# A two-block transformer layer on one core: the first feed-forward upward product as seven block products, staged through DRAM

## What is computed

```python
h = rmsnorm(x, g_ffn[i])                                              # 1024 x 1024
x = x + jnp.square(jax.nn.relu(h @ w_ffn_up[i])) @ w_ffn_down[i]      # up 1024 x 4096, down 4096 x 1024
```

## Time and profile before

| | us |
|---|---|
| three runs without profile | 3553.3, 3554.5 (median), 3556.45 |
| profiled execution, from first to last instruction (its own device time isn't listed apart) | 3550.2 |
| TensorE busy | 3451.9 (97%) |
| VectorE, ScalarE, GpSimd busy | 1781.8, 1286.5, 1058.5 |
| merge's last products end, first upward product starts | 1186.0 |
| the last downward products of this stage end | about 1884 |

### The profile page before, as it was taken

The page is one execution under the profiler, slowest core; times in us unless marked ns, Lnnn a source line. Parts: engine busy times, 40 slices in busy tenths (PEclk is TensorE's granted clock), DMA queues, the critical chain, the costliest instruction groups (busy, mean ns, idle before and its releaser), DMA issues.

```text
span 3550.2 us, 48554 instructions
## 1 busy us (share of the span) xinstructions
PE 3451.9 (97%) x20382; PEld 2810.6 (79%) x20382; DVE 1781.8 (50%) x2379; ACT 1286.5 (36%) x2195; POOL 1058.5 (30%) x594
## 2 busy tenths in 40 slices
PE   7999999999999999999998899999999999999999
PEld 6888888887678888888887677777788788888887
...
GB/s 151 40 24 43 47 25 46 51 34 7 1 175 181 54 48 48 49 53 48 48 48 89 101 81 81 81 80 107 175 205 148 90 48 48 48 49 52 48 48 54
DMA packets 280073, 253.14 MB, mean 71 GB/s; under 512 B 11365, under 2 KB 221729, under 8 KB 279856
## 3 DMA queue, kind: packets, MB, share of 16 engines
...
...
## 4 chain that ended last, share of the span: by engine, by line


## 5 line engine op out<-in xcount | busy, mean ns | idle before, releaser
L414 POOL TENSOR_TENSOR weight_lo<-stage,weight_hi 128x1024 fp32r<-128x1024 f32 (+4 forms) x267 | 628.6, 2359 | 1389.4 <-ACT weight_hi L406 1360.9
L377 PE MATMUL psum<-hT_hi,weight_hi 128*128 128x512 f32 x2240 | 884.3, 395 | 5.7 <-DVE hT_lo L563 4.2
L378 PE MATMUL psum<-hT_lo,weight_hi 128*128 128x512 f32 x2240 | 873.5, 390 | 0.0
L379 PE MATMUL psum<-hT_hi,weight_lo 128*128 128x512 f32 x2240 | 873.1, 390 | 0.0
L377 PEld LDWEIGHTS psum<-hT_hi,weight_hi 128*128 128x128 f32 x2240 | 421.7, 188 | 103.5 <-issue 5.2
L378 PEld LDWEIGHTS psum<-hT_lo,weight_hi 128*128 128x128 f32 x2240 | 421.8, 188 | 90.0 <-issue 4.1
L379 PEld LDWEIGHTS psum<-hT_hi,weight_lo 128*128 128x128 f32 x2240 | 421.5, 188 | 88.3
L406 ACT ACTIVATE weight_hi<-stage 128x1024 fp32r<-128x1024 f32 (+4 forms) x329 | 316.5, 975 | 477.8 <-PE psum L379 441.8
L2096 DVE TENSOR_TENSOR x<-x,psum 128x512 f32<-128x512 f32 x416 | 279.8, 687 | 218.8 <-PE psum L379 218.2
L377 PE MATMUL psum<-weight_hi,act_hi 128*128 128x512 f32 x864 | 338.9, 392 | 0.0
L379 PE MATMUL psum<-weight_hi,act_lo 128*128 128x512 f32 x864 | 338.7, 392 | 0.0
(11 more groups left out here) (379 smaller groups left out, 5280.1 us busy)
## 6 DMA issues: line engine op xcount, KB each, us to landing
stage<-in_w_in SPq DMA_DIRECT2D x64, 512.0 KB, 4.0
stage<-in_w_up SPq DMA_DIRECT2D x44, 512.0 KB, 3.9
scratch_gates<-gate ACTq DMA_DIRECT2D x64, 256.0 KB, 2.0
gs<-scratch_gates SPq DMA_DIRECT2D x64, 256.0 KB, 2.8
stage<-in_w_out SPq DMA_DIRECT2D x32, 512.0 KB, 4.7
stage<-in_w_ffn_up SPq DMA_DIRECT2D x32, 512.0 KB, 4.2
stage<-in_w_ffn_down SPq DMA_DIRECT2D x32, 512.0 KB, 3.7
stage<-in_w_down SPq DMA_DIRECT2D x22, 512.0 KB, 3.5
```

The source lines that it names most:

```text
L377: q.matmul(out, stat[0], mov[0], start=first, stop=False)
L378: q.matmul(out, stat[0], mov[1], start=False, stop=False)
L379: return q.matmul(out, stat[1], mov[0], start=False, stop=final)
L414: g.q.tensor_tensor(lo, K.staged(w), hi.bitcast(F32), ALU.subtract).then_inc(*S.w_lo_pool.up(w))
```

## The change

The stage is cut in two. All upward work comes first, and its result (relu squared, 16.8 MB) goes to a DRAM scratch `act1`; then all downward work, which fetches it back block by block (`act_fetch`).

The upward work goes by units of two blocks (256 hidden channels), 16 units. The normed input is a 2 x 2 matrix of quarters (512 channels by 512 tokens): B11, B21 of the first 512 tokens, B12, B22 of the others. The weights of a unit are four blocks too. A unit takes seven products of 512 channels, 128 outputs and 512 tokens (4 channel tiles times three matmuls, 12 each) in place of eight: P1, P6, P2, P7, P5, P4, P3. They multiply sums of weight blocks by sums of quarters. The sums of quarters T1 to T4 are made once (`dve_parts`, `act_parts`, `pool_parts`, `last_parts`); the sums of weight blocks for each unit by four VectorE operations on the staged tiles (`dve_weight_sums`), and they are split like other tiles. After P1, ScalarE copies the bank away (`kept`) and P2 goes on accumulating in it; VectorE joins P6, P7, P5, P4, P3 with what was kept (U2, U3, C22, C21, C12), ScalarE takes relu and square of the four results, SyncE stores them.

P1 and P2 of units 0 to 3 run ahead of all else (they need only B11 and B21); the weight tiles of these units are loaded twice. To make room, one ring slot of five is given up from the end of the merge to the end of the upward work, and the first three row tiles of x are stored to DRAM (`spill`) and come back behind the upward work (`x_back`); the first downward adds wait for them.

```diff
+OUTS, SPILL, EARLY = 4, 3, 4
...
+def sp_stage_load(K, r):
     sp, S = K.sp, K.S
-    if w >= STAGES:
-        if K.low[w - STAGES] == "G":
-            sp.wait_ge(S.w_lo_pool, w - STAGES)
-        else:
-            sp.wait_ge(S.w_lo_dve, w - STAGES)
-    src, shape = K.tiles[w]
-    sp.q.dma_start(K.staged(w).rearrange("p (k c) -> p k c", k=shape[1]), src).then_inc(*S.stage_load[w % STAGES].up(w, 16))
+    if r >= STAGES:
+        for what, i in K.load_uses[r - STAGES]:
+            if what == "low":
+                K.need_low(sp, i)
+            else:
+                sp.wait_ge(S.raw_sum, i)
...
+def dve_weight_sums(K, w):
+
+    v, S = K.v, K.S
+    f, u, _ = K.sums_of[w]
+    for r in K.load_of[w]:
+        v.wait_ge(S.stage_load[r % STAGES], r)
+    if u:
+        for before in K.unit_tiles[f, u - 1][1:]:
+            K.need_low(v, before)
+    else:
+        for t in range(SPILL):
+            v.wait_ge(S.spill, t)
+            v.wait_ge(S.xn, (K.up_norm[f], t))
+    c1, c2 = (K.staged(r) for r in K.load_of[w])
+    left, right = slice(0, HALF), slice(HALF, TILE)
+    v.q.tensor_tensor(K.sum1[:, :], c2[:, left], c2[:, right], ALU.add).then_inc(*S.raw_sum.up((f, u, 1)))
+    v.wait_ge(S.raw_sum, (f, u, 1))
+    v.q.tensor_tensor(K.sum23[:, left], K.sum1[:, :], c1[:, left], ALU.subtract).then_inc(*S.raw_sum.up((f, u, 2)))
+    v.q.tensor_tensor(K.sum23[:, right], c1[:, left], c2[:, left], ALU.subtract).then_inc(*S.raw_sum.up((f, u, 3)))
+    v.wait_ge(S.raw_sum, (f, u, 2))
+    v.q.tensor_tensor(K.sum4[:, :], c1[:, right], K.sum23[:, left], ALU.subtract).then_inc(*S.raw_sum.up((f, u)))
...
+def turn_bank(nid, t):
+    return "upper" if nid == 4 or (nid, t // (NT // 2)) == (3, 1) or (nid == 2 and t >= NT - 2) else "all"
...
+def act_turn_quarters(K, nid, t):
+
+    a, S = K.a, K.S
+    early = t < NT // 2
+    for k0, name, keep in ((0, "B11", "T2"), (4, "B21", "T4")) if early else ((4, "B22", "B22"),):
+        a.wait_ge(S.mm, ("turn", nid, t, k0))
+        a.q.activation(quarter(K, keep, t)[1], turned(K, nid, t, k0), ACT.Copy).then_inc(*S.hT_raw.up((nid, name, t)))
+        a.q.activation(quarter(K, name, t)[0][0], turned(K, nid, t, k0), ACT.Copy).then_inc(*S.hT_hi.up((nid, name, t)))
...
+def dve_parts(K, nid, t):
+
+    v, S = K.v, K.S
+    T1, T2, T3, T4 = (quarter(K, name, t)[1] for name in ("T1", "T2", "T3", "T4"))
+    v.wait_ge(S.hT_raw, (nid, "B11", t - NT // 2))
+    v.wait_ge(S.mm, K.up_after[nid])
+    v.wait_ge(S.mm, ("turn", nid, t, 0))
+    v.q.tensor_tensor(T1, turned(K, nid, t, 0), T2, ALU.subtract).then_inc(*S.part.up((nid, "T1", t)))
+    v.wait_ge(S.part, (nid, "T1", t))
+    v.wait_ge(S.hT_hi, (nid, "B22", t))
+    v.q.tensor_tensor(T2, turned(K, nid, t, 4), T1, ALU.subtract).then_inc(*S.part.up((nid, "T2", t)))
+    v.q.tensor_tensor(T3, quarter(K, "B22", t)[1], turned(K, nid, t, 0), ALU.subtract).then_inc(*S.part.up((nid, "T3", t)))
+    K.free(("turn", nid, t, 0), S.part)
+    K.free(("turn", nid, t, 4), S.part)
+    v.wait_ge(S.hT_raw, (nid, "B21", t - NT // 2))
+    v.wait_ge(S.part, (nid, "T2", t))
+    v.q.tensor_tensor(T4, T4, T2, ALU.subtract).then_inc(*S.part.up((nid, "T4", t)))
+    v.wait_ge(S.part, (nid, "T4", t))
+    dve_quarter_low(K, nid, "T2", t)
...
+PRODUCTS = {"P1": ("a", "B11", 0, 0, "P1"), "P6": ("b", "T2", 1, 0, "P6"), "P2": ("a", "B21", 0, 4, None),
+            "P7": ("b", "T3", 1, 4, None), "P5": ("c", "T1", 2, 0, "P5"), "P4": ("b", "T4", 2, 4, None),
+            "P3": ("c", "B22", 3, 0, None)}
+
+
+def unit_bank(f, u, name):
+    which = PRODUCTS[name][0]
+    return ("unit", which, f, u), (u % EARLY,) if which == "a" else (4 + u % 2 * 2 + (which == "c"),)
...
+    w = K.unit_tiles[f, u][part]
+    K.need_weight(w)
+    need_quarter(K, K.up_norm[f], moving)
+    if name == "P2":
+        pe.wait_ge(S.kept, (f, u))
+    elif name == "P7":
+        pe.wait_ge(S.joined, (f, u, "U2"))
+    elif name == "P4":
+        pe.wait_ge(S.joined, (f, u, "U3"))
+    elif name == "P3":
+        pe.wait_ge(S.joined, (f, u, "C22"))
+    hi, lo = K.weight(w)
+    for k in range(4):
+        mm = three(pe.q, b, (hi[:, k0 + k, :], lo[:, k0 + k, :]), [x[:, k, :] for x in K.q[moving]], first is not None and k == 0, k == 3,
+                   first is None)
+    mm.then_inc(*S.mm.up((name, f, u)))
...
+def dve_product(K, f, u, name):
+
+    v, S, key = K.v, K.S, ("unit", PRODUCTS[name][0], f, u)
+    kept, bank = K.kept[u % KEPT_ROWS], K.bank(key)
+    if name == "P6":
+        v.wait_ge(S.kept, (f, u))
+        v.wait_ge(S.mm, ("P6", f, u))
+        if u:
+            v.wait_ge(S.joined, (f, u - 1, "C12"))
+        v.q.tensor_tensor(K.U2[:, :], bank, kept[:, :], ALU.add).then_inc(*S.joined.up((f, u, "U2")))
+    elif name == "P7":
+        v.wait_ge(S.mm, ("P7", f, u))
+        v.q.tensor_tensor(K.U3[:, :], bank, kept[:, :], ALU.add).then_inc(*S.joined.up((f, u, "U3")))
+    elif name in ("P5", "P4", "P3"):
+        out, other = {"P5": ("C22", K.U3), "P4": ("C21", kept), "P3": ("C12", K.U2)}[name]
+        v.wait_ge(S.mm, (name, f, u))
+        v.wait_ge(S.joined, (f, u, "U3"))
+        if u:
+            v.wait_ge(S.act_store[out_slot(u, name)], (f, u - 1, name))
+        v.q.tensor_tensor(K.outs[out_slot(u, name)][:, :], bank, other[:, :], ALU.add).then_inc(*S.joined.up((f, u, out)))
+        if name != "P5":
+            K.free(key, S.joined)
...
+def sp_x_back(K, f, t):
+
+    sp, S, last = K.sp, K.S, UNITS_UP[f] - 1
+    for w in K.unit_tiles[f, last][1:]:
+        K.need_low(sp, w)
+    if t == SPILL - 1:
+        sp.wait_ge(S.joined, (f, last, "C12"))
+    sp.q.dma_start(K.x[:, t, :], K.dram["xs"][t]).then_inc(*S.x_back[t].up(f, 16))
+
+
+def sp_act_fetch(K, f, i):
+
+    sp, S = K.sp, K.S
+    u = i // 2
+    for name, (_, block, h) in OUTPUTS.items():
+        if unit_blocks(f, u)[block] == i:
+            sp.wait_ge(S.act_store[out_slot(u, name)], (f, u, name))
+    if i < 4:
+        sp.wait_ge(S.mm, ("P1", f, UNITS_UP[f] - 1))
+    else:
+        sp.wait_ge(S.act_lo, (f, i - 4, 1))
+    sp.q.dma_start(K.act_raw[i % 4][:, :], K.dram["act1"][i]).then_inc(*S.act_load[i % 4].up((f, i), 16))
+
+
+def act_act_fetch(K, f, i):
+    a, S = K.a, K.S
+    a.wait_ge(S.act_load[i % 4], (f, i))
+    if i < 4:
+        a.wait_ge(S.mm, ("P7" if i < 2 else "P5", f, UNITS_UP[f] - 1))
+    else:
+        a.wait_ge(S.mm, ("down", f, (i - 4) // GRP, NT - 1, 1))
+    a.q.activation(act_slot(K, f, i)[0], K.act_raw[i % 4][:, :], ACT.Copy).then_inc(*S.act_hi.up((f, i, 1)))
...
+    elif f == 1 and t < SPILL:
+        v.wait_ge(S.x_back[t], f)
...
+    for u in range(EARLY):
+        first(u)
+    for u in range(EARLY):
+        rest(u, True)
+    for u in range(EARLY, units):
+        first(u)
+        rest(u, False)
+
+    def product(u, name):
+        o.do("product", f, u, name)
+        if name in ("P2", "P7", "P4", "P3"):
+            o.released()
+    advance(norm, 1)
+    product(0, "P1")
+    o.do("parts", nid, 4)
+    product(1, "P1")
+    advance(norm, 1)
+    product(2, "P1")
+    o.do("parts", nid, 5)
+    advance(norm, 1)
+    finish(norm)
+    product(3, "P1")
+    o.do("parts", nid, 6)
+    product(0, "P2")
+    o.do("parts", nid, 7)
+    product(1, "P2")
+    for t in (4, 5):
+        o.do("last_parts", nid, t)
+    product(2, "P2")
+    for t in (6, 7):
+        o.do("last_parts", nid, t)
+    product(3, "P2")
+    for u in range(units):
+        for name in ("P1", "P6", "P2", "P7", "P5", "P4", "P3"):
+            if u >= EARLY or name not in ("P1", "P2"):
+                product(u, name)
+                if u == units - 1 and name in ("P2", "P7", "P4"):
+                    for i in {"P2": (0,), "P7": (1,), "P4": (2, 3)}[name]:
+                        o.do("act_fetch", f, i)
+    for t in range(SPILL):
+        o.do("x_back", f, t)
+    o.handover()
+    o.slot(RING - 1)
...
+        for n in range(2):
+            w = o.take(*rows512(down, n, GRP * g, GRP * (g + 1)))
+            for t in range(NT):
+                o.do("down", f, g, t, n, w)
+                if t == NT - 1:
+                    o.released()
+                o.do("down_rows", f, g, t, n)
+        for i in range(GRP * (g + 2), min(GRP * (g + 3), NF)):
+            o.do("act_fetch", f, i)
```

More of the change, by code:

```diff
@@ L538, in pe_turn @@
     for k0 in range(0, ND, 4):
-        b = K.open(("turn", nid, t, k0), "upper" if nid == 4 or (nid, t // (NT // 2)) == (3, 1) else "all")
+        b = K.open(("turn", nid, t, k0), turn_bank(nid, t))
         K.pe.wait_ge(K.S.xn, (nid, t))
@@ new lines, in unit_blocks, with pe_product @@
+def unit_blocks(f, u):
+    return (2 * u, 2 * u + 1) if f == 1 else (u, NF2 + u)
+def pe_product(K, f, u, name):
+    pe, S = K.pe, K.S
+    key, banks = unit_bank(f, u, name)
+    _, moving, part, k0, first = PRODUCTS[name]
+    b = K.open(key, banks) if first else K.bank(key)
+    w = K.unit_tiles[f, u][part]
[15 more added lines that the diff above has]
+    if name in ("P2", "P7", "P4", "P3"):
+        K.tile_done(w)
```

336 lines of the change are left out of this document (272 added, 64 removed).

## The result

| | before | changed |
|---|---|---|
| device time, median, us | 3554.4 (3553.3 to 3556.45, four runs) | 3574.5 (3572.87 to 3579.02, four runs) |
| ratio | | 1.0056, 95% interval 1.0042 to 1.0071 |
| profiled execution, span, us | 3550.2 | 3577.1 |
| first upward to last downward product, start to start, us | 1185.96 to 1885.66: 699.70 | 1195.27 to 1915.23: 719.96 |

The account below looks back on a forecast made before the run. TensorE, busy throughout the stage, was taken as the bound, so new waits add in full: -43.5 + 1 + 8.7 + 1 + 17 + 5.4 + 22.2 + 7.2 = +19.0 us on 3550.2. With 4.3 to the median: 3573.5, range 3555 to 3590.

Parts of the forecast that it names:

- The forecast's own case: Whole kernel: waits outweigh the saved matmuls, 3562 to 3590 us, chance 0.62.
- 192 matmuls: Upward work on TensorE: 1344 matmuls in place of 1536, at 0.2267 us each, 43.5 us less.
- turn 6 waits for T3 of row tile 5: Start of upward work: turn 6 needs banks that VectorE frees only with T3; 8.7 us of waiting.
- P6 of unit 0: Start of upward work: T2's low part of row tile 7 comes late for P6; 1 us (0 to 3).
- P7 of unit 0 behind the sums: First unit: P7 waits for U2, behind unit 1's weight sums on VectorE, which wait for GpSimd; 17 us.
- P7 of units 1 to 3: Early units: U2 comes late for P7, 2.2 us each in units 1 and 2, 1.0 in unit 3; 5.4 us.
- first wait of the boundary: Turn to downward work: block fetches on SyncE stand behind weight tiles' low parts; 13.1 us of waiting.
- x: Turn to downward work: x returns late and no downward bank is freed until then; 9.1 us more.
- cold starts: After four long waits TensorE starts at the lower clock level, 1.8 us each; 7.2 us (5 to 9).
- steady state: Later upward units: every product covers its join, P3 barely; taken as 0, with 0 to 6 us over 12 units.
- the rival with C22 1 us later: Steady state: C22 later than counted makes P3 wait in 12 units; +12 us, 3585 us, chance 0.15.
- The other sign: Turn to downward work: its waits are covered and two cold starts go, 25.8 us less, 3547.7 us; chance 0.08.

Follow-up runs that it names:

- g_twice: Changed kernel with P1 of units 4 to 15 computed twice into the same bank, 144 matmuls more; 3602.5 us.
- f_turn6: Changed kernel with the five quarter operations of row tile 5, T3 among them, ahead of the scaling of row tile 7; 3571.7 us.
- d_sums: Changed kernel with VectorE's weight sums of units 1 to 3 moved behind U2 of the unit before; 3566.1 us.
- a_fetch: Changed kernel with the first four fetches of finished blocks issued on SyncE right behind P1 of the last unit; 3554.1 us.
- k_hand: b_xback with the handover right behind the last P3, ahead of the casts and low parts of blocks 2 and 3; 3560.4 us.
- b_xback: Changed kernel with the three fetches of x moved earlier on SyncE, behind the stores of C22 and C21 of the last unit; 3570.05 us.
- h_join2: Changed kernel with VectorE computing C22 of units 4 to 15 twice before P3 may start; 3581.9 us.
- c_both: Changed kernel with the four block fetches behind P1 of the last unit and x fetched behind C21's store; 3549.8 us.
- j_best: Changed kernel with boundary fetches, start products, quarter operations and weight sums all reordered, nothing computed otherwise; 3536.1 us.

## Why the prediction was right

The forecast's own case came about: the places of the waits were right, and 3573.5 is 1.0 us off the median. Term by term, waits counted from start to start:

| term of the sum | predicted | measured |
|---|---|---|
| 192 matmuls | -43.5 | 144 more cost 32.64 (g_twice), 0.2267 each |
| P1 of unit 0 waits for a bank | 1 | 0.3 |
| turn 6 waits for T3 of row tile 5 | 8.7 | 8.4; 6.2 with T3 earlier (f_turn6) |
| P6 of unit 0 | 1 | 0.8 |
| P7 of unit 0 behind the sums | 17 | 14.8; 4.5 with the sums behind U2 (d_sums) |
| P7 of units 1 to 3 | 5.4 | 5.2 |
| first wait of the boundary | 13.1 | 13.9; 1.2 with the fetches ahead (a_fetch) |
| x | 9.1 | 10.5; gone in k_hand |
| cold starts (the lower clock level behind a wait) | 7.2 | 9.9 |
| steady state | 0 | 0.7, 0.06 a unit |

- **That the number came within 1 us is in part luck.** Five terms were 3.6 us too large together and four 5.6 too small. And the step from the span to the median did not hold: the median of before lay 4.3 us above its profiled span, that of the changed kernel 2.6 below. The span itself was forecast 19.0 us longer and came out 26.9 longer: 20.3 in the stage, 9.3 ahead of it, 2.7 less behind it. Of the 9.3, 5.1 had come about before the merge's first product (1048.06 against 1042.95), which lies between 1038.9 and 1048.3 in all traces.
- **What bounds it** was right, and the sum made over waits and a fixed price of a matmul therefore held. The 131 ns of the Trainium skill (TensorE: Matmul & The Clock Gate, Back-to-back issue gap) would have made the gain 25 us and g_twice 19; it came to 32.64, so here too the measurement decides against it.
- **P7 of unit 0**: the place in VectorE's queue was right, the size 2 us too large. The low part that the sums wait for ended 7.3 us after P6 did, not 8.7, and the four sums took 6.6, not 7.6: a pair that takes turns needs 1.65 to 1.7 us, where I had added up 1.29 and 0.6.
- **The boundary**: order on SyncE, as predicted. Of x only the first cause was seen. That x is fetched behind the fourth tile's low part, and that no bank is freed until it is back, is true, but VectorE's handover was met only 5.6 us before x landed (GpSimd's low part ended at 1567.9, the addition began at 1573.56), and b_xback ran into it.
- **Cold starts** were counted as four of 1.8; five waits were followed by the lower clock level, and the term was 2.7 us too small. Behind P7 of unit 2 a wait of 1.92 us was followed by 1.75 us of it.
- **Steady state**: the cover of 0.2 us that was counted is the distance from C22's end to P3's start, and 0.15 of it is there even when P3 waits (h_join2: C22 ends at 1500.13, P3 starts at 1500.28). The forecast of 0 held by nothing; one more operation brought 8.0 of the 12 us of the rival with C22 1 us later (h_join2).
- **Not in the sum**: turn 4, ahead of the first product, waits 4.80 us against 2.97. Both chains of statistics and scaling met a low part of GpSimd (before, the 2.15 us of the earlier trace rows; here, the scaling), but here VectorE makes a weight tile's low part (L462, 1179.67) ahead of the statistics, and before it made one behind the scaling (L422, 1176.80). The 1.8 us lie before the stage as measured here; that this order makes them was not tested.
- **The other sign** (boundary covered, 3547.7) had 0.08 and was refused for the kernel as it stands; c_both is that case by design, at 3549.8.

That VectorE and GpSimd take turns over operations with both inputs in SBUF carried 8 of the 17 us. It was not tested by itself, since no run takes one side away, and a pair needs a little less than the two alone (1.67 us from start to start, against 0.61 and 1.22). The rows of j_best, 0.68 against 1.77 us and 1.27 against 1.75 us for the same operations, agree with it, as does the rule of the Trainium skill (SBUF — State Buffer, SBUF: two separate sides) that was weighed in the prediction.
